# Delta layer of a two-layer trunk: the merging levels of the chunk inverse computed on parts of a tile

## The reference, cut to what matters

```
lower = where(strict, (k_beta @ k.T) * decay, 0)
sol = triangular_solve(lower + I, [v * beta, k_beta * exp(g)])    # unit lower triangular
u, w = split(sol)
# then, chunk after chunk:
v_new = u - w @ state
o = (q * exp(g)) @ state + (q @ k.T * decay) @ v_new
state = state * exp(g_last) + (k * exp(g_last - g)).T @ v_new
```

## Time and profile before

| | us |
|---|---|
| median of 3 runs | 2297.02 (2295.53 to 2299.01) |
| profiled execution | 2302.95 |
| its span, first to last instruction | 2301.2 |
| TensorE busy | 2248.0 (98%) |
| TensorE weight loads | 1875.7 (82%) |
| VectorE busy | 1400.3 (61%) |
| ScalarE busy | 1230.0 (53%) |
| GpSimd busy | 399.7 (17%) |

### The profile page before, as it was taken

How to read it: one execution, slowest core, us unless ns; L and a number is a source line. 1 busy time by engine, 2 the same in 40 slices (tenths; PEclk the granted TensorE clock), 3 DMA queues, 4 the chain that set the end, 5 groups by cost and what they waited for, 6 DMA issues and landing times. The chain is left out here.

```text
span 2301.2 us, 31341 instructions
## 1 busy us (share of the span) xinstructions
PE 2248.0 (98%) x11056; PEld 1875.7 (82%) x11056; DVE 1400.3 (61%) x2594; ACT 1230.0 (53%) x2509; POOL 399.7 (17%) x672
## 2 busy tenths in 40 slices
PE   7989999999999999999999999999999999999989
PEld 6768888888888888787888888888888888888877
DVE  5757667686867666576745738365482745738341
ACT  5646566566666665555545455454654545455430
POOL 1435161534425150560000000000000000000000
PEclk9999999999999999999999999999999999999999
DMA  4222232313222245585111121121111211121151
GB/s 142 46 51 62 62 80 59 83 37 79 49 67 60 58 101 181 185 272 191 54 38 56 28 57 46 38 65 38 47 37 47 65 38 56 28 57 46 54 217 51
DMA packets 301726, 174.26 MB, mean 76 GB/s; under 512 B 97228, under 2 KB 284004, under 8 KB 301572
## 3 DMA queue, kind: packets, MB, share of 16 engines
q1 hardware_dynamic: 301572, 172.26, 26.2%
HBM read 143.66 MB, written 28.56 MB: 75 GB/s over the span
## 5 line engine op out<-in xcount | busy, mean ns | idle before, releaser
L389 PE MATMUL b_front<-g_h_lo,wa_w_hi 128*128 128x512 f32 x2064 | 828.9, 402 | 0.0
L389 PE MATMUL b_front<-g_h_hi,wa_w_hi 128*128 128x512 f32 x2064 | 824.3, 399 | 4.4 <-PEq L1509 3.0
L389 PE MATMUL b_front<-g_h_hi,wa_w_lo 128*128 128x512 f32 x2064 | 824.7, 400 | 0.0
L389 PEld LDWEIGHTS b_front<-g_h_hi,wa_w_hi 128*128 128x128 f32 x2064 | 389.9, 189 | 81.7 <-issue 5.4
L389 PEld LDWEIGHTS b_front<-g_h_lo,wa_w_hi 128*128 128x128 f32 x2064 | 389.9, 189 | 77.5 <-issue 0.2
L389 PEld LDWEIGHTS b_front<-g_h_hi,wa_w_lo 128*128 128x128 f32 x2064 | 389.5, 189 | 76.4 <-issue 0.5
L2160 ACT ACTIVATE b_acc<-b_front,g_gains 128x512 f32<-128x512 f32 x96 | 66.1, 689 | 303.3 <-DVE b_qk L2464 213.3
L1266 DVE SCALAR_TENSOR_TENSOR a_acc<-a_x_raw,a_hw,a_acc 128x512 f32<-128x512 f32 x192 | 156.8, 817 | 6.8
L2338 DVE TENSOR_TENSOR wa_w_lo<-wa_raw,wa_w_hi 128x1024 fp32r<-128x1024 f32 x79 | 95.6, 1210 | 106.1 <-ACT wa_w_hi L2106 106.1
L772 POOL TENSOR_TENSOR a_bt<-a_bd,a_bx 128x112 f32<-128x112 f32 (+29 forms) x248 | 121.8, 491 | 213.7 <-DMA a_bd<-u_tiles 194.9
L775 POOL TENSOR_TENSOR a_bx<-a_bx,a_bt 128x112 f32<-128x112 f32 (+29 forms) x248 | 126.7, 511 | 19.4
(11 more groups left out here) (343 smaller groups left out, 4087.1 us busy)
## 6 DMA issues: line engine op xcount, KB each, us to landing
wa_raw<-in_b_w_in_dram SPq DMA_DIRECT2D x80, 512.0 KB, 3.9
wa_raw<-in_a_w_in_dram SPq DMA_DIRECT2D x48, 512.0 KB, 4.3
p_w_raw<-in_a_w_out_dram SPq DMA_DIRECT2D x40, 512.0 KB, 4.0
a_out<-a_og SPq DMA_DIRECT2D x64, 128.0 KB, 1.9
a_zx<-inverse_tiles SPq DMA_DIRECT2D x16, 384.0 KB, 4.7
p_a_raw<-a_out SPq DMA_DIRECT2D x40, 128.0 KB, 5.0
u_tiles<-a_u SPq DMA_DIRECT2D x8, 512.0 KB, 3.2
a_bd<-u_tiles SPq DMA_DIRECT2D x32, 128.0 KB, 3.6
```

Of the source, the lines that this page charges most:

```text
L389: last = pe.matmul(out, w[:, k, :], a[:, k, ks], start=(n == 0), stop=(n == 23))
```

## The change

The inverse is upper block triangular in one form, and its transpose is lower. The change computes only the parts that are not known to be zero or that somebody reads later, and keeps both forms in place:

- `zx` and `zf` become the two forms of a tile, each a tensor of its own; the block inverses are read back straight into them (with a wait for the last residual of the head before, which reads `zf`). `zx1` is gone.
- `um` holds level 0 only: half the elements, one mask.
- Level 0, first product: as before. Second product: for the form in `zf` the first 96 rows and last 96 columns (96 weight columns, 96 moving), for the transpose in `zx` the first 64 rows and columns (64 weight columns, 64 moving), in turn for e = 0 and 1. VectorE subtracts in two steps, 96 partitions by 192 elements and 64 by 128.
- Level 1: only the upper right 64x64 corner is made. The first product takes `corner[:, t]` as its weight, 128 rows by 64 columns, the transposed corner of u on partitions 64 to 127 with zeros above, and 64 moving columns of `zf`; ScalarE copies 64x128 elements; the second product has 64 rows, 64 weight columns and 64 moving; VectorE writes the corner of `zf` as minus the product (64x128).
- `corner` is made by four VectorE transposes a head (32 partitions, 8 tiles of 32 columns each), two in slot 28 and two in slot 30; TensorE waits for them (`corners`) before the first level-1 product of a head. Its zeros are written once in the setup.

```diff
@@ -359,6 +359,9 @@
 HALVES = 2 * UNITS
 LEVEL0 = 4
 LEVEL_STEP = 2 * LEVELS
+HB = P // 2
+FRONT3 = P - BLK
+CORNERS = (28, 30)
 DECAYS = (6, 9)
 CHAIN0 = 7
 SUMS = (9, 12, 15, 18)
@@ -451,7 +454,8 @@
         sq_hi = m_.sb("sq_hi", [P, HALF], F32R)
         sq_lo = m_.sb("sq_lo", [P, HALF], F32R)
         u = m_.sb("u", [P, T, P])
-        zx = m_.sb("zx", [P, T, 2, P])
+        zx = m_.sb("zx", [P, T, P])
+        corner = m_.sb("corner", [P, T, HB])
         zf = m_.sb("zf", [P, T, P])
         cols = m_.sb("cols", [P, 7, T, H])
         hc = m_.sb("hc", [P, 2, 6, T])
@@ -461,9 +465,8 @@
         bt = m_.sb("bt", [P, (BLK - PART) * PART])
         bxt = bd[:, 0:PART, :]
         dec = m_.sb("dec", [P, T, P])
-        um = m_.sb("um", [P, 2, 2, LEVELS, P])
+        um = m_.sb("um", [P, 2, 2, P])
         bc = m_.sb("bc", [P, 2, P])
-        zx1 = m_.sb("zx1", [P, 2, 2, P])
         state = m_.sb("state", [P, 2, DV])
         r = m_.sb("r", [P, DV])
         vn = m_.sb("vn", [P, DV])
@@ -525,7 +528,7 @@
         inv_out, inv_zero = sem("inv_out"), sem("inv_zero")
         back = [sem("back_first"), sem("back_rest")]
         bstep = sem("bstep")
-        zx_zero = sem("zx_zero")
+        zx_zero, corners = sem("zx_zero"), sem("corners")
         um_s, first_mm, first_c, lv_mm, lv_s = (sem(x) for x in ("um", "first_mm", "first_c", "lv_mm", "lv_s"))
         ks_mm, r_s, xr_mm, vn_s = sem("ks_mm"), sem("r_s"), sem("xr_mm"), sem("vn_s")
         osu_mm, o1_s, st_s, o_s = sem("osu_mm"), sem("o1_s"), sem("st_s"), sem("o_s")
@@ -637,7 +640,7 @@
 
             sp.wait_ge(zx_zero, 1)
             for c in range(2):
-                sp.dma_start(as_tiles(inv_dram[c]), zx[:, :, c, :]).then_inc(inv_zero, 16)
+                sp.dma_start(as_tiles(inv_dram[c]), zx[:, :, :]).then_inc(inv_zero, 16)
             sp.wait_ge(inv_zero, 32)
 
             def body(m, n, p):
@@ -717,16 +720,17 @@
                             sp.dma_start(as_blocks(inv_dram[1])[:, :, columns(q)], part_of(bx, q)).then_inc(inv_out, 16)
                             sp.dma_start(as_blocks(inv_dram[0])[:, columns(q)], part_of(bxt, q)).then_inc(inv_out, 16)
                         sp.wait_ge(inv_out, (n + 1) * (32 * PARTS_OF_BLOCK))
+                        sp.wait_ge(xr_mm, n * T)
                         for part, tiles in enumerate((slice(0, 2), slice(2, T))):
-                            for c in range(2):
-                                sp.dma_start(zx[:, tiles, c, :], as_tiles(inv_dram[c])[:, tiles]
+                            for c, form in enumerate((zf, zx)):
+                                sp.dma_start(form[:, tiles, :], as_tiles(inv_dram[c])[:, tiles]
                                              ).then_inc(back[part], 16)
 
             heads(sp, body)
 
         @block.gpsimd
         def _(pool):
-            pool.memset(zx[:, :, :, :], 0.0).then_inc(zx_zero, 1)
+            pool.memset(zx[:, :, :], 0.0).then_inc(zx_zero, 1)
             pool.wait_ge(cols_s, 1)
 
             def body(m, n, p):
@@ -737,8 +741,8 @@
 
                         pool.wait_ge(first_mm, m * (LEVELS * T // 2) + (LEVELS * max(b - 1, 0) + 1))
                         pool.wait_ge(ut, m * 4 + 2)
-                        pool.tensor_tensor(um[:, b % 2], spread(u[:, 2 * b:2 * b + 2, :], 2, LEVELS),
-                                           spread(g.level_mask[:, :, :], 1, 2), ALU.mult).then_inc(um_s, 1)
+                        pool.tensor_tensor(um[:, b % 2], u[:, 2 * b:2 * b + 2, :],
+                                           spread(g.level_mask[:, 0, :], 1, 2), ALU.mult).then_inc(um_s, 1)
                 if n is not None:
                     invert_blocks(n)
 
@@ -826,7 +830,10 @@
                         if 0 <= b < T // 2 and k in range(0, 2 * LEVELS, 2):
                             use = LEVELS * b + k // 2
                             act.wait_ge(first_mm, m * (LEVELS * T // 2) + (use + 1 + 1))
-                            act.activation(bc[:, :, :], first[:, :, :], ACT.Copy).then_inc(first_c, 1)
+                            if k:
+                                act.activation(bc[0:HB, :, 0:HB], first[0:HB, :, 0:HB], ACT.Copy).then_inc(first_c, 1)
+                            else:
+                                act.activation(bc[:, :, :], first[:, :, :], ACT.Copy).then_inc(first_c, 1)
                         t, k = divmod(s - CHAIN0, 3)
                         if 1 <= t < T and k == 0:
                             act.wait_ge(r_s, m * (T - 1) + t)
@@ -1106,7 +1113,6 @@
                         if 0 <= b < T // 2 and k < 2 * LEVELS:
                             level, second = divmod(k, 2)
                             use = LEVELS * b + level
-                            x = zx[:, 2 * b:2 * b + 2] if level == 0 else zx1[:, :, :, :]
                             if not second:
                                 pe.wait_ge(lv_s, m * (LEVELS * T // 2) + (use + 1))
                                 if level == 0:
@@ -1114,15 +1120,28 @@
 
                                         pe.wait_ge(back[b], m * 32 + 32)
                                     pe.wait_ge(um_s, m * (T // 2) + (b + 1))
+                                elif b == 0:
+                                    pe.wait_ge(corners, m * 2 + 3)
                                 for e in range(2):
-                                    last = pe.matmul(first[:, e, :], um[:, b % 2, e, level], x[:, e, 1], start=True, stop=True)
+                                    t = 2 * b + e
+                                    if level == 0:
+                                        last = pe.matmul(first[:, e, :], um[:, b % 2, e], zx[:, t], start=True, stop=True)
+                                    else:
+                                        last = pe.matmul(first[0:HB, e, 0:HB], corner[:, t], zf[:, t, HB:P],
+                                                         start=True, stop=True)
                                 last.then_inc(first_mm, 1)
                             else:
                                 pe.wait_ge(first_c, m * (LEVELS * T // 2) + (use + 1))
                                 for e in range(2):
-                                    last = pe.matmul(lev[:, e, 0], bc[:, e], x[:, e, 0], start=True, stop=True)
-                                    if level < LEVELS - 1:
-                                        last = pe.matmul(lev[:, e, 1], x[:, e, 0], bc[:, e], start=True, stop=True)
+                                    t = 2 * b + e
+                                    if level == 0:
+                                        pe.matmul(lev[0:FRONT3, e, 0, BLK:P], bc[:, e, 0:FRONT3], zf[:, t, BLK:P],
+                                                  start=True, stop=True)
+                                        last = pe.matmul(lev[0:HB, e, 1, 0:HB], zf[:, t, 0:HB], bc[:, e, 0:HB],
+                                                         start=True, stop=True)
+                                    else:
+                                        last = pe.matmul(lev[0:HB, e, 0, HB:P], zx[0:HB, t, 0:HB], bc[0:HB, e, 0:HB],
+                                                         start=True, stop=True)
                                 last.then_inc(lv_mm, 1)
 
             heads(pe, body)
@@ -1135,6 +1154,7 @@
                                   ALU.subtract).then_inc(w_low, 1)
 
             dve.memset(x_raw[:, 0:CONV - 1], 0.0).then_inc(convs, 1)
+            dve.memset(corner[0:HB, :, :], 0.0).then_inc(corners, 1)
             dve.memset(state[:, 1, :], 0.0).then_inc(setup, 1)
 
             for s_, c in ((act_out, 2), (o_s, 2), (og_s, T), (o1_s, 1), (vn_s, 1), (o_mm, 2),
@@ -1169,15 +1189,18 @@
 
             def merge(m, b, level):
                 use = LEVELS * b + level
-                x = zx[:, 2 * b:2 * b + 2] if level == 0 else zx1[:, :, :, :]
+                tiles = slice(2 * b, 2 * b + 2)
                 dve.wait_ge(lv_mm, m * (LEVELS * T // 2) + (use + 1))
                 if level:
                     dve.wait_ge(lv_s, m * (LEVELS * T // 2) + (use + 1))
                 if level < LEVELS - 1:
-                    dve.tensor_tensor(zx1[:, :, :, :], x, lev[:, :, :, :], ALU.subtract).then_inc(lv_s, 1)
+                    dve.tensor_tensor(zf[0:FRONT3, tiles, BLK:P], zf[0:FRONT3, tiles, BLK:P],
+                                      lev[0:FRONT3, :, 0, BLK:P], ALU.subtract)
+                    dve.tensor_tensor(zx[0:HB, tiles, 0:HB], zx[0:HB, tiles, 0:HB], lev[0:HB, :, 1, 0:HB],
+                                      ALU.subtract).then_inc(lv_s, 1)
                 else:
-                    dve.tensor_tensor(zf[:, 2 * b:2 * b + 2, :], x[:, :, 0], lev[:, :, 0],
-                                      ALU.subtract).then_inc(lv_s, 1)
+                    dve.tensor_scalar(zf[0:HB, tiles, HB:P], lev[0:HB, :, 0, HB:P], -1.0, None, ALU.mult
+                                      ).then_inc(lv_s, 1)
 
             def next_weight(n, s):
                 j = s // 6 + 1
@@ -1290,6 +1313,14 @@
```

(8 more changed lines are left out.)

## The result

| | before | after |
|---|---|---|
| median of 4 and 4 runs, us | 2298.02 (2295.53 to 2302.08) | 2311.07 (2308.4 to 2312.32) |
| ratio, 95% interval | | 1.0048 (1.0036 to 1.0061) |
| in a second set of runs (19 and 4) | 2298.29 | 2309.42; 1.0045 (1.003 to 1.006) |
| profiled execution, its span | 2302.95, 2301.2 | 2312.32, 2310.6 |

The change makes the kernel slower by 11 to 13 us, 0.5%. The shares of the whole don't explain this: TensorE is as busy as before in percent, and its weight loads and GpSimd have less to do.

A forecast was written before the change was run, and what follows sets the result against it. TensorE, busy 98% of the span, was taken as the bound: +17.8 us in its queue, less 4.8 and 1.8 of waits, gives +11.2 on 2297.0, so 2308.2 us; range 2303 to 2313.

The forecast's parts named there:

- 4 x 0.60: TensorE's level products: net +0.60 us for each pair of tiles, times 32 pairs +19.2 us.
- 0.20 (slot 6): Level-1 product directly behind L1078 in 7 heads: one way back to the full array (0.09+0.11) saved, -1.4 us.
- Pace of small records: TensorE's level products: 0.058 us per 64 by 64 record, 0.085 per 96 by 96, against 0.112 at full size.
- both sides are needed: TensorE records: weight and moving columns must both shrink, since a 128-column load sets the pace where the moving side is short.
- 96 columns count as full: Second product of level 0: 96 weight columns keep the full array's configuration, so four changes there and no extra 5.5 us.
- rival C's first half: Second product of level 0: 96 columns are their own configuration, +5.5 us; the whole rival up to 2318, chance 0.15.
- The excursion: TensorE going into 64 columns and back: 0.35 us, two drains of 0.09 each and weight loads in the open.
- Rival B: TensorE's configuration changes: only the drain is paid, loads being pulled ahead; 2289 us, chance 0.05.
- Wait (a): TensorE's wait at L983 of slot 8 for VectorE's merge: goes, -0.69 in 7 heads, -4.8 us.
- The 0.13 for which L1264 was to be held: VectorE's L1264 under GpSimd's um product: held 0.13 us instead of 0.75 once um is halved.
- Wait (b): TensorE's wait at L1118 of pair 2, level 1: covered by the 0.34 longer second product, -0.26 x 7 = -1.8 us.
- Transposes at 0.4, free: Four VectorE transposes a head, slots 28 and 30: 0.4 us each, fitting in idle time, costing nothing.

The follow-up runs named there:

- all 128: The kernel after with its new data flow, but every level product at 128x128: 0.9978 of before, 2295.05 us, a head 103.31.
- parts of 96: The kernel after, but no level product with fewer than 96 weight columns or 96 rows: 0.9938 of before, 2286.88 us, a head 102.11.
- Grouping: The kernel after with level 0's second product reordered, both 96-wide products first, then both 64-wide: 0.9992 of before, 2298.56 us.
- 64 rows: The parts of 96 kernel, but the second product of level 1 has 64 rows instead of 96: 0.9983 of before, 2295.36 us.
- parts of 68: The kernel after with 68 weight columns and rows in place of 64, the 96-column product kept: 0.9908 of before, 2279.43 us.
- mask of 512: The all 128 kernel, but GpSimd masks both levels in one step of 512 elements again: 0.9996 of before, 2299.94 us.
- experiment 6: The kernel after with each of the four transposes a head done four times, three into an unused tile: 1.0076 of before, 2317.3 us.

## Why the prediction was right

Forecast 2308.2 and +11.2 us; measured 2311.07 and +13.1 in one set, +11.1 in the other. One head of the loop by the prediction's terms: 4 x 0.60 - 0.20 (slot 6) - 0.69 - 0.26 = +1.25; measured +1.15. The level products alone come out as added up: against all 128, after is 2.04 longer a head, where 4 x 0.60 - 0.20 = 2.20 was worked out.

- *Pace of small records* (0.058 and 0.085): 0.056 to 0.061 for 64 and 68 wide, 0.083 to 0.085 for 96 wide. Right, and so is "both sides are needed": the record of 96 by 64 kept 0.085, the pace of its load.
- *96 columns count as full* (rival C's first half, +5.5): right. From L392 to L1138 (355.27 to 355.50) is the pace of a projection, 0.23, and parts of 96 have no drain. By the Trainium skill ("TensorEngine Tiling (Array Packing)", Available Configurations) the modes have 128, 64 and 32 rows and columns; the runs agree, with 68 and 96 in the full mode, which no row of before showed.
- *The excursion, 0.35 from one sighting of L952 and one of L1078*: right. L1138 to L392 is 1.12, and 0.11 follows in the late second load; 1.23 was worked out. Grouping shows it by time, 64 rows show it for rows.
- *Rival B, the drain without the loads*: 2289 did not come. Load and product start together at all four changes, so the rule of the Trainium skill by which loads are pulled ahead ("TensorE: Matmul & The Clock Gate", Part 2) didn't hold across a change of configuration; inside one (parts of 68, 0.0 idle) it did.
- *Wait (a), -0.69*: gone, by the cause given; the mask of 512 brings 0.5 back. The shorter merge (0.28 for 0.41) has the size of the rest, but no run has it alone. The 0.13 for which L1264 was to be held was wrong: with all 128 it is held 0.2 (0.68 for 0.48), and in after L1287 begins when GpSimd's step is nearly over, and isn't held at all.
- *Wait (b), -0.26*: gone, but the longer product is not the whole cause. From L1096 to L1016 are 1.36 us and 0.10 follows in the late second load; 0.90 + 0.23 by pace and 0.35 for the excursion are 1.48, so nothing of the wait is left. But with all 128, where no product is longer, only 0.10 of the 0.26 is left too (L1096 to L1016 1.44, less 1.34 by pace). The other 0.16 went with the new flow, and which part of it did that is open. Where TensorE comes earlier the wait is larger: 1.45 less 1.23 = 0.22 with parts of 96, 1.42 less 1.14 = 0.28 with parts of 68. The rows in after:

```profile
387.15 1.05 PE L1096 MATMUL b_front<-a_kq 128*128 128x128 f32 x8
388.14 0.45 PE L1130 MATMUL a_lev<-a_zf,a_corner 128*64 128x64 f32 x4
388.51 0.70 PE L1016 MATMUL a_step<-a_vn,a_kd 128*128 128x256 f32 x2
```

- *Transposes at 0.4, free*: 0.437 each, free, in head 0 too. But the reason was wrong. "No product of TensorE waiting on them in that slot" looked at TensorE in the same slot; the cover is SyncE's queue, one head long. Of the 2.6 us that experiment 6 added in slot 30 it held 0.9 to 2.2 in the six heads that lost time, an estimate (2.6 less the losses of 1.7 to 0.4), and not all of it, as the 3 us of VectorE's idle time behind the slot had made me expect.
- *The sum*: the two profiled executions of after have spans 9.4 and 6.7 above that of before, since stretches at a granted clock of 1.2 GHz, in which six or more projection records start 0.43 apart instead of 0.23 (1.2 us and more each), fall now here, now there. The sum is shown by the heads and by the medians, not by one span. From the first L1085 at 56 us to the record that starts at 1048.9 in before, which lies behind the last head, the two executions of after need 10.1 and 10.0 us more.

The kernel that beats both is the changed one with parts of 68: 0.9908 of before, 20 us less.

## What to carry to other kernels

Before a product is cut to 64 columns or rows, count how often the array's configuration changes around it: a way there and back cost 0.32 to 0.35 us here, and a 64x64 record saves 0.054. Cut to 68 or more (68 is the smallest size that ran here without a change), or put the small products side by side; the first gave 31 us against after, the second 12. And the cover of a step on a side engine is not the idle time behind it, but the slack of whatever queue waits for the next result of that engine; delay the step on purpose once and see where TensorE stops.

## What the runs showed of the chip that I had not expected

- 68 columns and 68 rows run without a change of configuration, at 0.06 us a record, nearly the pace of 64. Between 65 and 68 nothing was tried.
- A full weight load behind a record of 0.06 is 0.055 late though the configuration stays: two 256-wide products last 0.65 instead of 0.59.
- VectorE's first convolution step, begun under a step of GpSimd, ended 0.28 to 0.29 after it in all 20 cases of three kernels, after 0.50 to 1.24 us. In after it began 0.13 before GpSimd's end and took its undisturbed 0.48.
